# The mLSTM cell: key-value product as three fp32r products for three heads, ScalarE's work in another order, the samples' numerators made already turned

## The reference

```python
def step(carry, xs):
    cm, nv, m = carry
    ...
    w = jnp.exp(dlog - m_t[..., None])
    s_inter = jnp.exp(inter - m_t)
    qk = jnp.einsum('bthd,bshd->bhts', qc, kc) * w
    num = s_inter[..., None] * jnp.einsum('bthd,bhde->bhte', qc, cm) + jnp.einsum('bhts,bshe->bhte', qk, vc)
    den = s_inter * jnp.einsum('bthd,bhd->bht', qc, nv) + jnp.sum(qk, axis=-1)
    h = num / jnp.maximum(jnp.abs(den), jnp.exp(-m_t))[..., None]
    ...
    kw = kc * w_s.transpose(0, 2, 1)[..., None]
    c_new = dec[..., None, None] * cm + jnp.einsum('bshd,bshe->bhde', kw, vc)
    n_new = dec[..., None] * nv + jnp.sum(kw, axis=1)
```

## Time and profile before

| what | value |
|---|---|
| median of 3 runs | 2201.51 us (2201.0 to 2205.11) |
| profiled execution: own time, span of its instructions | 2201.16 us, 2199.4 us |
| granted TensorE clock, mean | 0.998 |
| busy share: TensorE, VectorE, ScalarE, GpSimd | 98%, 57%, 19%, 55% |
| the cell's groups, first to last head's "mean" | about 1317 to 1580 us |

### The profile page before, as it was taken

One profiled execution on the slowest core, in us unless ns is written; L12 is line 12 of the kernel. 1 busy time (PEld: TensorE's weight loads), 2 busy tenths in 40 slices (PEclk: granted clock), 3 DMA queues, 4 the chain that ended last, 5 costly groups with the idle time before them and its releaser, 6 DMA issues. The chain is left out here.

```text
span 2199.4 us, 38981 instructions
## 1 busy us (share of the span) xinstructions
PE 2156.8 (98%) x15839; PEld 2019.4 (92%) x15839; DVE 1244.7 (57%) x2095; ACT 423.2 (19%) x780; POOL 1203.1 (55%) x1228
## 2 busy tenths in 40 slices
PE   9989899999999999999999999999999999999998
PEld 9988789989999999999999995587699999999997
DVE  6888875454625344676557645772754364435263
ACT  6224541222000000121202113421422220000002
POOL 7675666526656655666657650032254365665663
PEclk9999999999999999999999999999999999999999
DMA  6224344212222222224433323552332122222221
GB/s 219 77 87 145 112 144 192 78 39 78 77 95 78 77 82 89 76 92 153 152 145 136 142 100 141 203 192 78 120 137 75 39 79 95 77 79 94 77 78 62
DMA packets 41809, 235.95 MB, mean 107 GB/s; under 512 B 4672, under 2 KB 10048, under 8 KB 16584
## 3 DMA queue, kind: packets, MB, share of 16 engines
q1 hardware_dynamic: 24512, 157.57, 20.2%
q10 hardware_dynamic: 17160, 76.38, 9.1%
HBM read 200.05 MB, written 33.89 MB: 106 GB/s over the span
## 5 line engine op out<-in xcount | busy, mean ns | idle before, releaser
L501 POOL TENSOR_TENSOR wlo<-raw,whi 128x512 fp32r<-128x512 f32 (+1 forms) x684 | 827.4, 1219 | 112.6 <-ACT whi L1253 69.9
L494 POOL TENSOR_SCALAR whi<-raw 128x512 fp32r<-128x512 f32 x512 | 365.3, 714 | 824.1 <-PE psum L596 771.3
L596 PE MATMUL psum<-xnh,whi 128*128 128x288 f32 (+1 forms) x2784 | 607.6, 296 | 13.2 <-DVEq L210 3.6
L596 PE MATMUL psum<-xnh,wlo 128*128 128x288 f32 (+1 forms) x2784 | 603.9, 295 | 0.0
L596 PE MATMUL psum<-xnl,whi 128*128 128x288 f32 (+1 forms) x2784 | 603.8, 295 | 0.0
L596 PEld LDWEIGHTS psum<-xnh,whi 128*128 128x128 f32 x2784 | 451.9, 189 | 20.4 <-issue 11.8
L596 PEld LDWEIGHTS psum<-xnh,wlo 128*128 128x128 f32 x2784 | 451.8, 189 | 0.0
L596 PEld LDWEIGHTS psum<-xnl,whi 128*128 128x128 f32 x2784 | 451.8, 189 | 0.0
L596 PE MATMUL psum<-hh,whi 128*128 128x288 f32 x992 | 212.0, 295 | 2.1 <-DVE hl L2330 2.1
L596 PE MATMUL psum<-hl,whi 128*128 128x288 f32 x992 | 211.8, 294 | 0.0
L596 PE MATMUL psum<-hh,wlo 128*128 128x288 f32 x992 | 210.7, 293 | 0.0
(11 more groups left out here) (459 smaller groups left out, 2766.1 us busy)
## 6 DMA issues: line engine op xcount, KB each, us to landing
raw<-in_w SPq DMA_DIRECT2D x145, 1024.0 KB, 4.8
C<-in_C ACTq DMA_DIRECT2D x4, 1024.0 KB, 4.8
o_cp<-mvt ACTq DMA_DIRECT2D x4, 1024.0 KB, 3.9
o_cs<-C ACTq DMA_DIRECT2D x4, 1024.0 KB, 6.5
t_xc<-xc ACTq DMA_DIRECT2D x3, 1152.0 KB, 7.3
t_z<-mv ACTq DMA_DIRECT2D x3, 1152.0 KB, 4.1
t_q<-mq ACTq DMA_DIRECT2D x3, 1152.0 KB, 4.2
t_k<-mk ACTq DMA_DIRECT2D x3, 1152.0 KB, 4.2
```

The lines of the kernel that those rows point to most:

```text
L494: pool.tensor_scalar(whi[:, s, c], raw[:, s, c], 1.0, 1.0, ALU.mult, ALU.mult).then_inc(S("slab_hi"), 1)
L501: ins = pool.tensor_tensor(wlo[:, s, c], raw[:, s, c], whi[:, s, c].bitcast(F32), ALU.subtract)
L596: ins = pe.matmul(bank(g, 2 * m + b)[:, 0:t1 - t0], W[wi][:, kk, m0 + m, :], r[:, kk, t0:t1], start=(at_first and wi == 0 and r is rh), st ...
```

## The change

Four things are changed, all in the cell.

1. "kv" is made of three fp32r products for the first, second and last head (`CELL_SPLIT = (4, 4, 0, 4)`). GpSimd splits the turned v into the first four tiles of `xnh` and `xnl` and the turned k into `mkt_high`, which lies over `mv`, and `mkt_low`, which lies over `mkt`: 16 operations of 128x512 for a head. The loop now runs over token blocks j outside and over banks d inside, and waits for the split of each j.
2. The samples' numerators come turned out of TensorE: the state C0 is the stationary operand and `qs` moves. ScalarE's copy of them and the four transposes are gone. In "den", the sums over `wt` now stand ahead of what needs `qs`, `wts` and C0.
3. ScalarE evicts the turned k before `high_y` of tiles 0 and 1, and reads "den" before `high_y` of tiles 2 and 3 and before its sums.
4. As `mkt_high` lies over `mv`, the next head's `mv` is loaded only when "kv" is done. (Semaphores are also renamed or reused: `x_again`, `bank_read`.)

VectorE's stream keeps its instructions in their order.

```diff
+            def cell_split(n):
+                m, at = CELL_SPLIT[n], 4 * CELL_SPLIT_BY[n]
+                pool.wait_ge(S("cell_vt"), n + 1)
+                for j in range(m):
+                    pool.tensor_scalar(mv_split(j)[0], mvt[:, j, :], 1.0, 1.0, ALU.mult, ALU.mult).then_inc(S("cell_split"), 1)
+                for j in range(m):
+                    pool.wait_ge(S("cell_split"), at + m + j)
+                    hi, lo = mv_split(j)
+                    pool.tensor_tensor(lo, mvt[:, j, :], hi.bitcast(F32), ALU.subtract).then_inc(S("cell_split"), 1)
+                at += 2 * m
+                pool.wait_ge(S("cell_kt"), n + 1)
+                for j0 in range(0, m, 2):
+                    for j in (j0, j0 + 1):
+                        pool.tensor_scalar(mkh[:, j, 0:ML_DH], mkt[:, j, :], 1.0, 1.0, ALU.mult, ALU.mult).then_inc(S("cell_split"), 1)
+                    for j in (j0, j0 + 1):
+                        pool.wait_ge(S("cell_split"), at + 2 * j0 + 2 + (j - j0))
+                        pool.tensor_tensor(mkl[:, j, :], mkt[:, j, :], mkh[:, j, 0:ML_DH].bitcast(F32), ALU.subtract).then_inc(S("cell_split"), 1)
...
+            for n in range(first // 2 * 2, third // 2 * 2):
+                split(n % 2, n // 2)
+                if n == first:
+                    cell_split(0)
+                    cell_split(1)
+                if n == SL["ml_out", 0, 0]:
+                    cell_split(3)
...
                 g, B = open_("den")
                 pe.wait_ge(S("cell_pt"), n + 1)
-                pe.wait_ge(S("cell_qs"), n + 1)
-                pe.wait_ge(S("cell_smp"), n + 1)
-                pe.wait_ge(S("cell_c"), 16 * (n + 1))
-                for d in range(ML_T):
-                    mm(B[2][0:TS, :], qs[:, d, :], C0[:, d, :], d == 0, False)
-                mm(B[2][0:TS, :], wts[:], vt5[:], False, True).then_inc(S("bank_filled"), 1)
                 for j in range(NTB):
                     mm(B[0][:, P * j:TP], ones[:], wt[:, blk(j):blk(j) + TP - P * j], j == 0, j == NTB - 1)
+                pe.wait_ge(S("cell_qs"), n + 1)
                 for d in range(ML_T):
                     mm(B[1][:, 0:TS], n0b[:, d, :], qs[:, d, :], d == 0, False)
+                pe.wait_ge(S("cell_smp"), n + 1)
                 mm(B[1][:, 0:TS], ones[0:TS, :], wts[:], False, True)
-                pe.wait_ge(S("bank_read"), n + 1)
+                pe.wait_ge(S("cell_c"), 16 * (n + 1))
                 for e in range(ML_T):
-                    ins = pe.transpose(B[3][:, TS * e:TS * e + TS], tm[0:TS, 1, P * e:P * e + P], ident[0:TS, 0:TS])
+                    out = B[3][:, TS * e:TS * e + TS]
+                    for d in range(ML_T):
+                        mm(out, C0[:, d, P * e:P * e + P], qs[:, d, :], d == 0, False)
+                    ins = mm(out, vt5[:, P * e:P * e + P], wts[:], False, True)
...
-                for d in range(ML_T):
-                    for j in range(NTB):
-                        ins = mm(B[d], mkt[:, j, P * d:P * d + P], mvt[:, j, :], j == 0, j == NTB - 1)
...
+                m, at = CELL_SPLIT[n], 4 * CELL_SPLIT_BY[n] + 2 * CELL_SPLIT[n]
+                for j in range(NTB):
+                    if j < m:
+                        pe.wait_ge(S("cell_split"), at + 2 * (j - j % 2) + 3 + j % 2)
+                    for d in range(ML_T):
+                        c = slice(P * d, P * d + P)
+                        if j < m:
+                            hi, lo = mv_split(j)
+                            ins = mm(B[d], mkh[:, j, c], hi, j == 0, False)
...
+                            mm(B[d], mkl[:, j, c], hi, False, False)
+                            ins = mm(B[d], mkh[:, j, c], lo, False, j == NTB - 1)
+                        else:
+                            ins = mm(B[d], mkt[:, j, c], mvt[:, j, :], j == 0, j == NTB - 1)
```

More of the change, by code:

```diff
@@ L41 @@
 OUT_BEFORE = ("num", "kv", "kvs", "mean")
+CELL_SPLIT = (4, 4, 0, 4)
+CELL_SPLIT_BY = [sum(CELL_SPLIT[:n]) for n in range(ML_H + 1)]
 CELL_STEPS = ("smp", "kT", "den", "num", "kv", "kvs", "mean")
@@ L1686, in _ @@
                     load(mk[:], A["t_k"][nxt], "cell_k")
[L1687 to L1693 removed]
                 g = GR["cell", h, "kv"]
                 group_ready(act, g)
+                if nxt is not None:
+                    load(mv[:], A["t_v"][nxt], "cell_v")
                 for d in range(ML_T):
```

44 lines of the change are left out of this document (25 added, 19 removed).

## The result

| kernel | median, us | runs | ratio to the kernel before, 95% interval |
|---|---|---|---|
| before | 2202.39 (2201.0 to 2205.11) | 5 | |
| changed | 2217.11 (2214.83 to 2225.16) | 5 | 1.0073 [1.0061, 1.0085] |

The change makes the kernel slower by 0.7%, 14.7 us. I had forecast 2205.9 us, with a range up to 2212: the sign was right, the time lies outside the range. The profiled execution's span is 2215.3 us.

A forecast was written before the change was run, and what follows sets the result against it. TensorE was taken to set the pace, with VectorE next, 3.95 us behind in slack. Heads of -3.4, +3.5, -0.1 and +4.7 us sum to +4.7 us, giving 2205.9 us, range 2196 to 2212.

The forecast's parts named there:

- The fp32r triple: "kv" as 48 fp32r matmuls takes 10.9 us against 13.9, 2.9 us less TensorE work in each of three heads.
- The turns: GpSimd's splits alternate with thirteen VectorE operations reading SBUF, which then take 20.1 us instead of 11.7: 8.4 us a head.
- the cost of the samples' numerators: In each head, 40 short passes of 4.7 to 5.0 us replace 4.9 us of products and transposes: -0.1 us.
- my -3.4: First head: splits meet no VectorE work, so TensorE keeps its gain, -2.9 - 0.1 - 0.4 = -3.4 us.
- the wait for C0: First head's "den": C0 is needed some 3.5 us later, so its 1.42 us wait goes; -0.4 us, bounds 0 and 1.4.
- a wait of 6.4 us: Second head, ahead of "kvs": TensorE would be there at 1416.7 but waits for VectorE until 1423.1.
- my +3.5: Second head: VectorE finishes the samples' state at 1428.1 instead of 1424.66, and the next "score" waits for it.
- +4.7: Last head: VectorE's turns with GpSimd delay the mean's subtraction from 1580.32 to 1585.0, and TensorE waits for that chain.
- ScalarE's order: Reading |den| sooner removes waits; y's later high parts cost nothing if VectorE is late anyway, up to 1 us otherwise.
- Rival 1: VectorE and GpSimd hardly meet, so "kvs" begins 3.5 us sooner in three heads: -10.6 us, 2190.6 us; chance 0.12.
- Rivals 2 and 3: Turns cost half, 4.2 us a head (2197 us, chance 0.18), or whole GpSimd operations (2213.7 us, chance 0.15).
- Rival 4: The fp32r triple in "kv" saves nothing, so the first head gives back 2.9 us: 2208.8 us; chance 0.05.

The follow-up runs named there:

- the run with memsets: The changed kernel with the samples' numerators made as before and GpSimd's splits writing constants, reading nothing; 2202.47 us, ratio 0.9994.
- ScalarE's order alone: The changed kernel without fp32r products and with the samples' numerators made as before, leaving ScalarE's order and mv's late load; 2206.04 us, ratio 1.0009.
- the passes mixed: The changed kernel with its short passes spread out, ten behind each wide product; 2225.63 us, ratio 1.0118.
- the run with two waits: The kernel before with VectorE's division repeated in the second and last head, so that TensorE waits; 2214.87 us, ratio 1.0048.
- the run with old numerators: The changed kernel with the samples' numerators made as before, with ScalarE's copy and four transposes; 2218.16 us, ratio 1.0059.
- the first head alone with C0 needed later: The kernel before with fp32r "kv" in the first head only and the samples' products behind two wide ones; 2198.65 us, ratio 0.9984.

## Why the prediction was wrong

**What held.** The fp32r triple: "kv" takes 11.3 us, from 1411.63 to the start of "kvs" (10.9 forecast), with no wait in it. The turns: 7.5 us in the second head where I had 8.4 (of which 0.16 is a slip: 0.04 us added to 1.75 is 1.79, not 1.81), and the run with memsets points to the reading of SBUF. That "num" is read within 0.3 us of the forecast is in part luck: VectorE began its run 0.75 us later than before and was 0.9 us quicker in it than I had. The sign of the whole held, but not by the waits that I had it from.

**The step that failed** is the cost of the samples' numerators: "40 passes are 4.7 to 5.0 us. I take -0.1 us a head, bounds -0.2 and +0.1." It priced the passes by rows of eight at full clock and asked only for their own length. That was short by 0.8 us (5.6 us for four tiles where I had at most 5.0); and the clock falls to half with them, for 3 to 10 us. Alone they cost the cell 344.89 - 333.26 = 11.6 us beside ScalarE's order alone, 2.9 a head (some 1 us more if the slow scores, which only the second of the two traces has, are taken out). In the changed kernel the first head misses my -3.4 by 2.5 us: 0.8 for the passes' own length, 1.65 for "num" (10.55 instead of 8.90), 0.4 for "kv", less 0.3 as the wait for C0 gave back more than I took. The third loses 3.3 us to them (105.06 with the order alone, 108.41 here, 104.41 with the passes mixed).

**A second step was wrong and hidden.** "So its gain becomes a wait of 6.4 us" takes a wait as worth its length. Where it occurs it costs over twice that: 8.7 us for 3.67 in the run with two waits. In the changed kernel the slow "num" fills that wait in the second head. Its +2.6 us is near my +3.5 since VectorE is as late as forecast and the next "score" waits 0.43 us for it; that TensorE would stand idle before that was wrong, and where it does, in the run with old numerators, the head takes 59.76 us. In the last head what remains of it, 1.36 us, brings a second slow stretch: +6.7 instead of +4.7.

**A third, small one:** ScalarE's order, which I costed at nothing in the third head. TensorE waits 1.20 us there for y; the part is 1.4 us longer.

By these steps: first head +2.5, second -0.9, third +4.8, last +2.0 beside the forecast, 8.4 us together; the forecast's 4.7 and these make the 13.0 measured in the cell. The remaining 1.7 us of the difference in medians is within what executions differ by elsewhere (the two traces differ by 1.7 us ahead of the cell and by 1.2 behind it).

**The rivals.** None was right. Rival 1 had TensorE unhindered; the run with memsets shows what that was worth, 2.9 us in the cell and not 10.6, since ScalarE's order then costs VectorE 2.75 us and the third head its 1.5, the last head's "kvs" waits 1.32 us, and the first head's scores ran slow. Rivals 2 and 3 priced the thirteen operations at 4.2 and 12.3 us more than before, where 7.5 was measured: whole instructions of the other engine aren't paid for. Rival 4 fell with "kv" at 11.3 us. The missing rival was the clock, though the profile of before offered no row below 1.00 in the cell to find it by.

## What to carry to other kernels

A piece of work on the engine that sets the pace has two prices: its own length, and the clock that it leaves behind. Read the granted clock by windows after each change in the shape of matmuls or in a wait, and where short products can't be avoided, put them between wide ones: here that was worth 0.6% with the same work (ratio 1.0059 to 0.9995). And before speeding up the bound engine, count the slack of the next: here it was 3.95 us, which two tiles of four kept within in the second head and four did not; no kernel with products in more than the first head measured faster than before. The best version, the first head alone with C0 needed later, is 0.16% faster than before (ratios 0.9984 and 0.9983, with both intervals below 1); the changed kernel is 0.7% slower.

## What the runs showed that I had not expected

- The clock falls with TensorE busy for all of the time: 40 passes of 64 columns with ten more ahead of them, then 0.50 for 10 us in which it is busy for 10 us. Where eight were left it stayed at 1.00, and so it did with all 50 in groups of ten, in 15 of the 16 heads of four runs.
- Waits of like length differ, even in one place: 1.19, 1.35 and 1.36 us ahead of "kvs" in the last head were followed by a slow stretch from within "kvs" on (4.90, 5.83 and 5.26 us), 1.32 us in the run with memsets by none:

```profile
1573.61 3.70 PE L667 MATMUL psum<-vt,kt 64*128 64x512 f32 x8 [1.32 <-DVEq L212]
```

- The first head's scores, behind a wait of 0.75 to 0.79 us in all traces, lose 1.7 us to the clock in twelve of twenty traces. What decides it stays open.
- The run with old numerators (waits of 4.00 and 6.75 us, no short passes) and the changed kernel (short passes, a wait of 1.36 us) have ratios of 1.0059 and 1.0073, and curing the passes alone gave no shorter cell (347.17 us, 345.60 in the changed kernel): two causes that lie in one place hide one another.
- Six of eighteen kernels lose some 9 us from the norm on, by a stop on TensorE (4.6 to 5.9 us) and the slow clock behind it, more than 300 us behind all edits, each with nine more packets of the queue that loads instructions than its neighbours.
